# The front's weight chunks and the transposed input in one run for each partition, in a one-core decoder layer kernel

## The reference: what is computed

```
proj  = x @ W_in + b_in                      # 5192 columns: q, k, v, indexer q/k/weights, conv in, two gates
y_attn = sparse_attention(q, k, v, top-64 keys by the indexer, bias by distance) @ W_o_attn
y_conv = silu(LN(depthwise_conv31(GLU(conv_in)))) @ W_o_conv
mix   = (sigmoid(g_attn) * y_attn + sigmoid(g_conv) * y_conv) @ W_out
x     = LN(alpha * x + mix)
h     = alpha * x + MoE(x)                   # 32 experts, 4 for each token, clamped SwiGLU
out   = LN(h + sigmoid(h @ W_pg) * (p @ W_pp))
```

## Time and profile before

| | |
|---|---|
| median of 3 runs | 1175.01 us (1174.99 to 1175.03) |
| span of the profiled execution | 1173.0 us; the page gives no other time of that execution, and the runs' median lies 2.0 us above the span |
| TensorE (PE) busy | 1134.9 us, 97% |
| HBM to the core over the span | 381 GB/s; 430 GB/s where the experts run |
| DMA queue q1 (SP) | 52704 packets, 439.79 MB |
| DMA queue q10 (ACT) | 7552 packets, 7.38 MB |

### The profile page before, as it was taken

The page is one execution under the profiler, slowest core; times in us unless marked ns, Lnnn a source line. Parts: engine busy times, 40 slices in busy tenths (PEclk is TensorE's granted clock), DMA queues, the critical chain, the costliest instruction groups (busy, mean ns, idle before and its releaser), DMA issues.

```text
span 1173.0 us, 13754 instructions
## 1 busy us (share of the span) xinstructions
PE 1134.9 (97%) x5620; PEld 573.9 (49%) x5620; DVE 299.7 (26%) x775; ACT 173.6 (15%) x336; POOL 11.4 (1%) x26
## 2 busy tenths in 40 slices
PE   9999999999999999999889999999999989999997
PEld 7888888734344343434234343443434333334346
DVE  0639842521113111111110211121111111111126
ACT  1213230211111111101010111111111010111112
POOL 0110000000000000000000000000000000000000
PEclk9999999999999999999999999999999999999999
DMA  9996367599999999999999999999999999999970
GB/s 319 353 325 233 109 276 297 217 405 377 430 430 430 431 428 431 429 430 430 429 426 428 430 423 433 429 432 426 434 430 430 430 429 429 423 428 427 425 329 37
DMA packets 60328, 448.16 MB, mean 382 GB/s; under 512 B 6656, under 2 KB 35616, under 8 KB 40544
## 3 DMA queue, kind: packets, MB, share of 16 engines
q1 hardware_dynamic: 52704, 439.79, 90.4%
q10 hardware_dynamic: 7552, 7.38, 1.9%
HBM read 444.53 MB, written 2.62 MB: 381 GB/s over the span
## 4 chain that ended last, share of the span: by engine, by line
PE 78%; DMA 18%; DVE 2%; ACT 1%; issue 1%; SPq 0%; ACTq 0%; DVEq 0%
PE bank L441 45%; DMA arena<-in_w_gu 17%; PE bank L711 10%; PE bank L460 5%; PE bank L418 4%; PE bank L858 2%; PE bank L871 2%; PE bank L1253 2%; PE bank L447 2%; ACT arena L1435 1%; PE bank L784 1%; DMA arena<-in_w_in 1%; PE bank L435 1%; PE bank L1126 1%; PE bank L1186 0%
## 5 line engine op out<-in xcount | busy, mean ns | idle before, releaser
L441 PE MATMUL bank<-arena 128*64 128x512 f32 x3168 | 695.3, 595 | 18.7 <-DMA arena<-in_w_gu 16.3
L441 PEld LDWEIGHTS bank<-arena 128*64 128x64 f32 x3168 | 233.8, 137 | 443.2 <-issue 407.0
L480 DVE TENSOR_TENSOR arena<-bank,arena 128x512 f32<-128x512 f32 x33 | 22.8, 692 | 685.7 <-PE bank L447 685.6
L711 PE MATMUL bank<-arena 128*128 128x256 f32 (+1 forms) x544 | 117.8, 377 | 0.5 <-DMA arena<-in_w_in 0.5
L711 PEld LDWEIGHTS bank<-arena 128*128 128x128 f32 x544 | 101.9, 190 | 15.0 <-DMA arena<-in_w_in 1.1
L1435 ACT ACTIVATE arena<-bank 128x512 f32<-128x512 f32 x62 | 37.0, 597 | 402.8 <-PE bank L441 402.8
L460 PE MATMUL bank<-arena 64*128 64x512 f32 x272 | 67.8, 616 | 0.7 <-ACT arena L1438 0.7
L418 PEld LDWEIGHTS bank<-sel,arena 128*128 128x128 f32 x480 | 54.7, 192 | 11.4 <-issue 11.4
L418 PE MATMUL bank<-sel,arena 128*128 128x128 f32 x480 | 57.6, 278 | 0.0
L1438 ACT ACTIVATE arena<-bank 128x512 f32<-128x512 f32 x32 | 19.1, 597 | 210.3 <-PE bank L441 210.3
L1636 DVE SCALAR_TENSOR_TENSOR arena<-arena 128x256 f32<-128x256 f32 x120 | 48.5, 479 | 0.5 <-DVE arena L1636 0.2
(11 more groups left out here) (213 smaller groups left out, 477.4 us busy)
## 6 DMA issues: line engine op xcount, KB each, us to landing
arena<-in_w_gu SPq DMA_DIRECT2D x45, 4096.0 KB, 31.2
arena<-in_w_dn SPq DMA_DIRECT2D x60, 2048.0 KB, 33.3
arena<-in_w_gu SPq DMA_DIRECT2D x33, 2048.0 KB, 38.7
arena<-in_w_in SPq DMA_DIRECT2D x19, 1024.0 KB, 12.8
arena<-in_w_gu SPq DMA_DIRECT2D x9, 1024.0 KB, 9.1
arena<-in_w_dn SPq DMA_DIRECT2D x6, 1024.0 KB, 9.9
arena<-in_w_out SPq DMA_DIRECT2D x4, 1024.0 KB, 5.1
arena<-in_w_pg SPq DMA_DIRECT2D x2, 2048.0 KB, 32.4
```

The lines of the kernel that those rows point to most:

```text
L441: mm = pe.matmul(to[half * CAP:(half + 1) * CAP, :], rows, w[:, half * 512:(half + 1) * 512], start=first, stop=last)
L711: mm = pe.matmul(bank[n % 4][:, lo:S], w[:, k, j * P:(j + 1) * P], xT_sb[:, k, lo:S], start=(k == 0), stop=(k == KD - 1))
```

## The change

The host stores W_in, W_o_attn, W_o_conv and W_out chunk after chunk, and inside a chunk partition after partition, so that the 8 KB that a partition reads of a chunk lie in one piece (2304 bytes for chunk 2). The kernel's load of a chunk has then one run for each partition, in place of eight runs of 1 KB (288 bytes for chunk 2; four runs of 2 KB for W_o_attn and W_o_conv). The four quarters of chunk 0 and of xT have one run of 2 KB for each partition in place of two of 1 KB. What stands in SBUF afterwards is the same. The order of the instructions on every engine, all waits and semaphores, the ring and the DMAs of all other inputs are as before; no DMA is added or removed.

```diff
--- before.py
+++ after.py
@@ -295,6 +295,13 @@
 
         src = {"in": w_in, "oa": w_oa, "oc": w_oc, "out": w_out}
 
+        def chunk_runs(i):
+
+            what, _, n = FRONT[i]
+            size = (4 if what in ("oa", "oc") else KD) * n
+            at = P * sum((4 if w in ("oa", "oc") else KD) * m for w, _, m in FRONT[:i] if w == what)
+            return src[what][at:at + P * size].rearrange("(p m) -> p m", p=P), size
+
         def wait_chunk(eng, i):
 
             eng.wait_ge(arrived[i % NS], 16 * (i // NS + (i % NS > 0)))
@@ -569,10 +576,10 @@
             def _(sp):
 
 
-                what, c0, n = FRONT[0]
+                size = KD // 4 * FRONT[0][2]
                 for quarter in range(4):
-                    sp.dma_start(w_view(0)[:, 2 * quarter:2 * quarter + 2, :],
-                                 src[what][2 * quarter * P:(2 * quarter + 2) * P, c0:c0 + n].rearrange("(k p) c -> p k c", p=P)
+                    sp.dma_start(wslot(0)[:, quarter * size:(quarter + 1) * size],
+                                 w_in[quarter * P * size:(quarter + 1) * P * size].rearrange("(p m) -> p m", p=P)
                                  ).then_inc(first_in[quarter], 16)
                 def early(n, piece=None):
                     load_pair(sp, n, n // CPE, n % CPE, piece)
@@ -581,16 +588,14 @@
                     sp.wait_ge(*front_used(i + (0 if piece == 0 else 1)))
                     early(n, piece)
 
-                for i, (what, c0, n) in enumerate(FRONT):
-                    if i == 0:
-                        continue
+                for i in range(1, NF):
                     if i == 25:
                         sp.wait_ge(lg_out, 8)
                         early(7)
                     if i >= NS:
                         sp.wait_ge(*front_used(i - NS))
-                    sp.dma_start(w_view(i), src[what][:, c0:c0 + n].rearrange("(k p) c -> p k c", p=P)
-                                 ).then_inc(arrived[i % NS], 16)
+                    runs, size = chunk_runs(i)
+                    sp.dma_start(wslot(i)[:, 0:size], runs).then_inc(arrived[i % NS], 16)
 
                 into_ring(0, 17)
                 sp.dma_start(wpp, w_pp.rearrange("(k p) d -> p k d", p=P)).then_inc(ple_in, 16)
@@ -1298,7 +1303,7 @@
 
                 for quarter in range(4):
                     a.dma_start(xT_sb[:, 2 * quarter:2 * quarter + 2, :],
-                                xT[2 * quarter * P:(2 * quarter + 2) * P, :].rearrange("(k p) t -> p k t", p=P)
+                                xT[quarter * P:(quarter + 1) * P, :].rearrange("p (k t) -> p k t", k=2)
                                 ).then_inc(xT_in[quarter], 16)
                 a.dma_start(relb_sb[:, :], relb).then_inc(relb_in, 16)
                 a.dma_start(oneh_sb[:, :], onehot).then_inc(relb_in, 16)
@@ -1953,13 +1958,23 @@
         a = _np.asarray(a)
         return a.reshape(2, P, 4, -1).transpose(0, 2, 1, 3).reshape(a.shape)
 
+    def chunk_major(what, a):
+
+        a = _np.asarray(a)
+        pieces = []
+        for i, (w, c0, n) in enumerate(FRONT):
+            if w == what:
+                k = 2 if i == 0 else a.shape[0] // P
+                pieces.append(a[:, c0:c0 + n].reshape(-1, k, P, n).transpose(0, 2, 1, 3).reshape(-1))
+        return _np.concatenate(pieces)
+
     b = _np.asarray(b_in[0])
     placed = [b[c:c + n] for c, n in ((QI0, 512), (Q0, 512), (K0, 512), (CA0, 512), (CG0, 512), (GA0, D), (GC0, D))]
     given = {
-        "x": by_rows(x[0]), "xT": _np.asarray(x[0]).T, "pT": _np.asarray(p[0, 0]).T, "w_in": w_in[0],
+        "x": by_rows(x[0]), "xT": _np.asarray(x[0]).T.reshape(4, 2, P, S).transpose(0, 2, 1, 3).reshape(4 * P, 2 * S), "pT": _np.asarray(p[0, 0]).T, "w_in": chunk_major("in", w_in[0]),
         "bT": _np.concatenate([rows(a) for a in placed], axis=1),
         "bki": _np.concatenate([b[KI0:WI0], b[KI0:WI0]])[:, None], "b_in": b,
-        "w_oa": w_o_attn[0], "w_oc": w_o_conv[0], "w_out": by_rows(w_out[0]),
+        "w_oa": chunk_major("oa", w_o_attn[0]), "w_oc": chunk_major("oc", w_o_conv[0]), "w_out": chunk_major("out", by_rows(w_out[0])),
         "dwT": _np.asarray(w_dw[0]).T.reshape(4, P, CW).transpose(1, 0, 2).reshape(P, 4 * CW),
         "convT": _np.concatenate([rows(a[0]) for a in (b_dw, conv_ln_g, conv_ln_b)], axis=1),
         "ln1T": _np.concatenate([rows(turned_rows(a[0])) for a in (ln1_g, ln1_b)], axis=1),
```

## The result

The changed kernel takes 1193.41 us (median of 4 runs, 1192.74 to 1194.23) against 1175.0 us: a ratio of 1.0156, 95% interval 1.0144 to 1.0169. The forecast was 1194.0. The time came out, and so did its cause, a second queue that starves; the place where TensorE pays for it did not, as the rows show.

The account below looks back on a forecast made before the run. TensorE nearly bounds the front and DMA the experts. A 17.6 us TensorE shift behind the table plus 1.4 us of slower clock gave 19.0 on 1175.0, so 1194.0 us; its own range 1189 to 1200, the whole range 1173.5 to 1200.

Parts of the forecast that it names:

- Bounds, and the shift through to the end: Front nearly bound by TensorE, experts by DMA; a TensorE shift in the front reaches the end one for one.
- One packet in turn: DMA engines alternate one packet each of SP's and ScalarE's queues; ScalarE's packet waits 310 ns instead of 47.
- The price of 8 KB: An 8 KB weight packet takes one DMA engine 0.31 us, bounded above by 0.38.
- The number of turns: On each engine, 8 packets per chunk; the table's first packet is ScalarE's 177th behind xT, and its write has 64.
- The gain at the start: Chunk 1 lands at about 12.0 instead of 12.97 us, between 0 and 1.7 us gained.
- Issues take no time of ScalarE: ScalarE's DMA issues: queued transfers do not block it; it stands at `tab_out` until 60 us, TensorE before tile 10.
- How long SP stays full: SP's weight queue never runs dry until chunk 17 lands at 51.6 us; the table then lands near 60.
- The clock: After TensorE's gap at tile 10, half speed over 3 us costs about 1.4 us, added once.
- No queueing: Rival for the queues: turns go by bytes or small packets slip through; 1174.0 us, chance 0.13.
- Turns of 4 KB: Rival for the queues: an 8 KB piece counts as two turns; 4.5 us less, 1189.5 us, chance 0.08.
- dearer: Rival for weight loads: 8 KB packets cost 0.38 us, chunk 17 lands 9 us later; 1202 to 1203 us, chance 0.03.
- a real gain: Rival in the front: faster chunks let something later start earlier, over 2 us in all; 1172.0 us, chance 0.06.

Follow-up runs that it names:

- e3: Full change, but each contiguous chunk stored block by block, so each partition reads eight 1 KB runs; against the kernel before: 1175.11 us, ratio 0.9999.
- e4: Full change, but each partition's part of a chunk in two runs of 4 KB; against the kernel before: 1193.32 us, ratio 1.0152.
- e5: Full change, but each partition's part of a chunk in four runs of 2 KB; against the kernel before: 1175.20 us, ratio 1.0000.
- e9: Full change, SP holding chunk 6 onward for the table's write and chunk 9 onward for its reads; against the kernel before: 1175.20 us, ratio 0.9999.
- e6: Full change, with wr stored as one 1 KB run per partition instead of eight of 128 bytes; against the kernel before: 1195.74 us, ratio 1.0178.
- e7: Full change, with thirteen small loads moved from ScalarE's queue to SP's, behind chunks 1 and 11; against the kernel before: 1178.04 us, ratio 1.0025.
- e11: Full change with all chunks in 2 KB runs and the small loads on SP's queue; against the kernel before: 1174.34 us, ratio 0.9988.

## Why the prediction was right, and where it was not

- *Bounds, and the shift through to the end.* Right. 17.46 us at chunk 5, 17.45 at the first expert, 17.9 on the span. The profiled run is the fastest of the four, 17.7 us above before; their median is 18.4 above.
- *One packet in turn.* Right: 115 to 115 with 8 KB beside 128 bytes, 112 to 109, and 17 to 17 in 0.3 us, which rules out the coarser grain of whole groups that was weighed. The counts were forecast to stay equal to 50 us; they did until SP's queue ran dry, near 46. e3, e4 and e5 vary the packet, e9 its rival for turns.
- *The price of 8 KB.* Right. From 20 to 40 us SP's queue moved 8.00 MB in 1097 turns (below), 976 of 8 KB; 20 x 16 / 976 = 0.33 us, with the partners, where 0.32 was taken.
- *The number of turns.* Counted short on both sides. Each DMA has one packet more on each engine than it has data (I take it for its completion), and this takes a turn too: 9 for a chunk and not 8, and up to the table's write 292 for ScalarE's queue, not 272. More partners and more to carry; nearly the same moment.
- *The gain at the start.* Wrong in size: 1.0 us was taken, and chunk 1 began 0.23 us later than before (13.24, 13.01). The step "xT and chunk 0 together gain 0.5", for which no row stood, left out that SP's queue is ahead of ScalarE's by then, so that xT's last quarter already takes turns with chunk 1's 8 KB (TensorE waits for in_xT at 10.91, and from 8 to 9 us SP's packets are of 8 KB: 49 of them, 0.39 MB). It did not matter to the sum, as said there.
- *Issues take no time of ScalarE.* This is the step that failed, a term put at nothing without a reason. The working let "bgu, x and pT" and the table simply stand in the queue, and put the wait at `tab_out`. The queue takes only so much: the issues blocked, ScalarE's evacuations stood behind them, and TensorE lost its time at chunk 3 and at the small transposes, from 22 us on, where the forecast had it wait from 45 on. The sum survived, since both places pay for the same thing, a queue of ScalarE's that moves one packet for each large one of SP's until SP's is dry. In e4 and e6, where the blocks are shorter, the wait is where the forecast had it, 15.6 and 18.2 us. That the sum survived so closely is luck.
- *How long SP stays full.* Forecast to 51.6 us with 17 chunks. TensorE stopped earlier, so only chunks 0 to 15 (16.02 MB) went out, the queue ran dry near 46, and the table landed at 55.9 for 60. The router's weights landed after 36.8 us, as the signs had it.
- *The clock.* Under-sized. 1.4 us for one gap; the trace has several. Chunk 3 took 3.0 us more at the lower level, and from the transposes to chunk 4 it took 3.8 us where it had 1.7, of which 0.6 was a wait: about 4.5 in all. The waits before them are 6.4 + 5.4 + 0.6 = 12.4. That is 16.9 of the 17.5 us; the rest is the later start and small gaps. The forecast had 17.6 of waiting and 1.4 of clock. So the 0.6 us by which the total was missed (18.4 between the medians for 19.0) flatters it: one term 5 us too large and one 3 us too small made up for most of each other, and the profiled run lies 0.7 us under the median besides.
- *The rivals.* "No queueing" is excluded by the counts. "Turns of 4 KB" for an 8 KB packet is excluded by them too, since it needs two packets of ScalarE's for each of SP's. Its sum, 1189.5, fits the real 4 KB packets of e4, which took 1193.3. What it missed there: the table landed at 57.6 for 55.5, as completions took turns too, and chunk 6, after the wait, took 9.71 us where e5 has 7.14, 2.6 for the 1.4 of clock. Neither "dearer" nor "a real gain" shows.

## What to carry to other kernels

Making one queue's packets larger is not free for the other queue. Before it is done, count the packets for each engine of whatever shares the engines, small ones above all, multiply by the time of the new packet, and see what waits for the last of them and how long the large queue stays full. What helped here was to put small loads that something early depends on into the queue of the large ones (e7, and without loss e11), to hold the large ones back until the small are through (e9), or to keep the packets at 2 KB (e5). And a stall that is removed in front of such a contention may come back behind it, as in e6.

## What the runs showed of the hardware

**A completion takes a turn.** SP's queue from 20 to 40 us in the kernel after, and ScalarE's from the start until the table had landed:

```profile
q1 hardware_dynamic: 1097, 8.00, 95.8%
```

```profile
q10 hardware_dynamic: 4672, 4.76, 24.7%
```

8.00 MB are 976 pieces of 8 KB; the row has 1097, 9/8 of that. And 4672 packets are 292 for each engine: the 272 of data that the prediction counts, xT's 32 with them, and one for each of 20 DMAs. I take the one packet more of each DMA for its completion; the counts show that it is there and takes a turn, not what it is. For a DMA with 8 pieces the completion is one turn in nine, against one in 65 with 1 KB pieces.

**An issue can block the engine that issues.** In the kernel after, q10's packets that had begun when the issue of br ended (24.34 us), and when that of pT ended (38.11 us):

```profile
q10 hardware_dynamic: 1459, 1.44, 17.4%
```

```profile
q10 hardware_dynamic: 2221, 1.53, 12.8%
```

For one engine that is 91 and 139 packets. Issued by then, completions included, were 175 and 227, of which 9 and 17 are the DMA's own. So 75 and 71 were outstanding ahead of it when ScalarE was let go. It isn't a simple limit: bgu's issue, straight behind ln1_col's, took 0.3 us with over 80 ahead. What exactly is counted stays open; no run was made for it.

**From 4 to 8 KB the loss did not grow.** 1, 2, 4 and 8 KB packets in SP's queue gave 1175.1, 1175.2, 1193.3 and 1193.4 us. With 2 KB the table landed at 41.9 us, just inside its cover. With 4 KB it went in turns to its end, with SP's queue still full, and landed at 57.6. With 8 KB the turns were slower, but SP's queue ran dry first and the rest went alone, to land at 55.9 and in e6 at 60.9. Either way the landing comes when nearly all that the two queues had to move by then is through: 21.9, 20.8 and 22.9 MB. That 4 and 8 KB agree to 0.1 us isn't explained by this, since they lost their time at different places; it is shown for these two sizes and this kernel alone.
